# Queries as two single-pass products of a rounded copy and its rest, penalties in single passes, and the first gate sums behind tile 17 of the z projection

## The chip, the cores and the metric

The kernel runs on one core of a Trainium2 chip. The core has TensorE (PE in the profile), VectorE (DVE), ScalarE (ACT), GpSimd (POOL), SyncE (SP, which here only issues transfers) and 16 DMA engines. The metric is the device time of one execution in microseconds (us); less is better.

## The reference

One inference step of one decoder layer, for a prompt of 256 rows and for 8 samples with 2,048 past tokens each. Cut to what matters:

```python
z = x @ w_in                        # (264 rows) x (1024 x 3072); columns q | k | v | B | C | h
# sample: keys and values of 16 pages of 128 tokens, 8 heads x 64
gate = einsum('bthd,bnhd->bthn', q, kmean)       # one number per block of 256 tokens
sel  = top_k(gate, 3)                            # attend to the 3 best blocks and the own one
s = q . k / 8 - slopes * distance;  s = -inf outside sel
att = softmax(s) @ v
mix = concat(att, B * dwconv3(C * h)) @ w_out
x1 = LayerNorm(alpha * x + mix)
u  = dwconv3(x1 @ w_ffn_up);  a, g = split(u)
y  = LayerNorm(alpha * x1 + (silu(a) * g) @ w_ffn_down)
```

Outputs are y, the new keys and values and the last rows of both convolutions.

## The kernel before, in words

Five programs, one for each engine, are written out by hand. Within an engine or a queue everything happens in the written order, and semaphores with thresholds tie the engines together, so a wait holds back all that is written behind it.

**z projection.** TensorE computes 24 tiles of z, `z_tile(0)` to `z_tile(23)`. A tile is 8 fp32 products of 128x264; a fp32 product shows as two matmuls in the profile. Four tiles share one chunk of `w_in` (2 MB), and the chunks take turns in the two halves of `wring`. ScalarE copies each tile out of PSUM (`s_ze`) and issues the next chunk when a half is free. From tile 8 on two PSUM banks take turns, so `z_tile(n)` waits for the copy of tile n-2.

**Sample queries.** TensorE computes the query rows `qs` of the 8 samples first. `query(b)` spreads sample b's row over all partitions, as a product of `qs` (512 columns) with a column of the selector `sel`, and ScalarE copies it to `qb`. Queries 2 to 7 stand in pairs behind tiles 0, 1 and 2.

**Key scan.** A "page group" j = 0 to 31 is four pages (1 MB) of keys in one of four slots of `KV`; j = 4b + s belongs to sample b. VectorE multiplies it with the query (`multiply`, L907) and sums over each head (`reduce`, L917). `scan(j)` is `multiply(j+1)` and then `reduce(j)`. For the groups in `POOLED` GpSimd does the last page's product (`multiply_page`, L541), and except for the groups in `WHOLE` ScalarE sums the last page (`sum_products`, L643). SyncE loads group j into its slot when group j-4 has been multiplied.

**Gate and softmax of samples 0 to 3** (`x = 0`), woven into z tiles 16 to 22. It is a chain that goes back and forth between engines: `gate_sums(0)` on TensorE (16 products with one column each, L1439, needs `reduce(15)`), `gate_penalties(0)` on VectorE (L958 to L966), `penalties(0)` on TensorE (two fp32 products of 512 columns, L1450 and L1452), `token_max(0)` on VectorE (L975, L976), `max_rows(0)`, `max_diagonal(0)`, `max_broadcast(0)`, `shifted_scores(0)`, `exponentials(0)` on ScalarE, `probability_sums(0)` on VectorE, `denominators(0)` on TensorE and then VectorE, and the weights `Pw` for the values. Samples 4 to 7 (`x = 1`) follow the same steps near 193 us.

**Prompt heads.** `head_scores(i)` (TensorE), `head_masked(i)` (VectorE), `head_exp(i)`, `head_normalise(i)` (ScalarE), `head_transposes(i)` and `head_outputs(i)` for head pairs i = 0 to 3 stand between the z tiles as well.

**SyncE's queue.** It issues the key pages, then value pages in between. The first value group that lies in `wring` waits for all 24 z tiles, because the last chunk of `w_in` lies there:

```python
elif i >= 4:
    sp.wait_ge(s_z, 24)
```

In the written order, this wait stands behind `load_keys(6, 0)` (group 24), and that one needs `multiply(20)` on VectorE and `multiply_page(20)` on GpSimd. Behind it stand all other keys and values, the `w_ffn_up` pieces and everything else that is loaded.

**After z.** TensorE takes up `values` (L1547), `mix_tile` and the row tiles, then `x1` and an early part of the up projection, until the last value group (31) has been used. Then x1 is split into a rounded part and its rest, and the remaining up and down projections run as three single-pass (fp32r) products for each fp32 one, to the end.

Of the kernel before, what the change touches and what calls it, by code (L numbers as in the profile page):

```python
# [59 lines left out]
def build(nc, x_prompt, x_sample, cache_k, cache_v, state_conv, state_ffn_conv, page_table,  # L60
# [13 lines left out]
    with ctx:  # L74
        def sb(name, shape, dt=F32):
            return ctx.enter_context(nc.sbuf_tensor(name, shape, dt))[:]

        def at(name, offset, shape, dt=F32R):
            return nc.alloc_sbuf_tensor_at(name, shape, dt, offset=offset)[:]

        def sem(name):
            return ctx.enter_context(nc.semaphore(name))
# [14 lines left out]
        lnT = sb("lnT", [P, 16])  # L97
        xsP = sb("xsP", [P, KT, 32])
        uptail = sb("uptail", [P, NTAIL, 2 * FT])
        cst = sb("cst", [P, 2 * FT, NS])  # L100
        smax = sb("smax", [P, 32])
        msum = sb("msum", [P, 32])
# [3 lines left out]
        G8 = sb("G8", [32, NBLK])  # L106
        beats = sb("beats", [32, NBLK, 2, NBLK])
        pen = sb("pen", [32, NBLK])
        penx = sb("penx", [32, NBLK, 32])
        tri = sb("tri", [32, NBLK * NBLK])  # L110
        sel = sb("sel", [P, NS])
        qkT = sb("qkT", [P, 4, NS])
# [7 lines left out]
        shift = sb("shift", [P, 3])  # L120
        nhalf = sb("nhalf", [P, 3])
        alibi = sb("alibi", [P, NPAGE * NH])

        T = sb("T", [P, 2, NPAGE + 1, 4 * NH])
        wlo0_mem = nc.sbuf_base - NS * (NPAGE + 1) * NH * 4
# [9 lines left out]
        hT0 = sb("hT", [P, 2, 3 * P])  # L135
        cu = sb("cu", [P, NPR])
        old = at("old", nc.sbuf_base - NPR * 4, [P, 2 * FT, NS], F32)
        ct = sb("ct", [P, NPR])
        dist = sb("dist", [P, 3 * P])
        cs2 = at("cs2", nc.sbuf_base - 3 * P * 4, [P, 2 * FT, NS], F32)  # L140
# [59 lines left out]
        first_rows = ((P, ps[:, 2:4, :], 0, rows[:, 0, :]), (P, ps[:, 0:2, :], P, rows[:, 1, :]),  # L200
                      (NS, ps[0:NS, 4:6, :], NPR, srows[0:NS, :]))

        s_id = sem("ident_landed")
        s_xs = sem("x_sample_landed")
        s_sel = sem("selector_landed")
        s_pad = sem("x_sample_padding")
# [303 lines left out]
        def _(pool):  # L510
# [18 lines left out]
                chain(nc.gpsimd.tensor_tensor(dst, old_rows(0, 2 * FT, k), taps(0, 2 * FT, k), ALU.mult))  # L529
            chain(nc.gpsimd.tensor_tensor(cst, cst, old, ALU.add))  # L530
            pool.sem_inc(s_cst, 1)

            def multiply_page(j):
                b, s = divmod(j, SLOTS)
                pool.wait_ge(s_qb, b + 1)
                pool.wait_ge(s_kv[s], 16 * GP * b + 16 * GP)
                if j - 2 in WHOLE:
                    pool.wait_ge(s_red, j - 1)
                else:
                    pool.wait_ge(s_reda, act_sums(j - 1))  # L540
                nc.gpsimd.tensor_tensor(prod[:, j % 2, GD * DA:GP * DA], kv[:, s, GD, :], qb[:, b, :], ALU.mult).then_inc(s_kpool, 1)  # L541
# [23 lines left out]
            nc.gpsimd.tensor_copy(vsT, zT[:, 8:12, NPR:R]).then_inc(s_vst, 1)  # L565
            multiply_page(19)
            for t in range(4):
                if t in (1, 2, 3):
                    multiply_page(19 + t)
                pool.wait_ge(s_ze, 20 + t + 1)  # L570
                nc.gpsimd.tensor_tensor(catT[:, 4 + t, 0:NPR], catT[:, 4 + t, 0:NPR], zT[:, 12 + t, 0:NPR], ALU.mult).then_inc(s_cvT, 1)
            nc.gpsimd.tensor_tensor(catT[:, 4:8, NPR:R], cus, zT[:, 12:16, NPR:R], ALU.mult).then_inc(s_cvT, 1)

            for j in range(23, 30):
                multiply_page(j)
# [48 lines left out]
        def _(act):  # L624
# [131 lines left out]
            head_exp(3)  # L756
            z_tile(19)
            act.dma_start(wo_mix, wout[:, 4:KT, :]).then_inc(s_wom, 16)
            head_normalise(3)
            exponentials(0)  # L760
            z_tile(20)
            sum_products(19)
            kv_rows(1)
            z_tile(21)
            kv_rows(3)
            z_tile(22)
            head_transposes(2)
# [114 lines left out]
        def _(dve):  # L882
# [436 lines left out]
        def _(pe):  # L1319
# [39 lines left out]
            def query(b):  # L1359
                if b >= 2:  # L1360
                    pe.wait_ge(s_qb, b - 1)
                nc.tensor.matmul(ps[:, 4 + b % 2, :], sel[:, b:b + 1].to_broadcast([P, P]), qs,  # L1362
                                 start=True, stop=True).then_inc(s_qbps, 1)

            def z_tile(n, between=None):
                c, i = divmod(n, 4)
# [76 lines left out]
            def penalties(x):  # L1443
                pe.wait_ge(s_pen, x + 1)
                if x == 0:
                    pe.wait_ge(s_ownT, 4)
                else:
                    pe.wait_ge(s_r1, KT)
                distances = alibi.rearrange("p (g o h) -> p g o h", g=NPAGE, o=1).to_broadcast([P, NPAGE, 4, NH])
                nc.tensor.matmul(ps[:, 4, :], ident, distances, start=True, stop=False)  # L1450
                blocks = penx.rearrange("q k (o m) -> q k o m", o=1).to_broadcast([32, NBLK, 2, 32])
                nc.tensor.matmul(ps[:, 4, :], ones[0:32, :], blocks, start=False, stop=True).then_inc(s_penps, 1)  # L1452

            def max_rows(x):
                pe.wait_ge(s_pm, x + 1)
# [51 lines left out]
            head_transposes(1)  # L1507
            z_tile(16)
            head_scores(3)
            gate_sums(0)  # L1510
            z_tile(17)
            penalties(0)
            z_tile(18)
            max_rows(0)
            z_tile(19, lambda: max_broadcast(0))
            z_tile(20)
            denominators(0)
            kv_rows(1)
            z_tile(21)
            kv_rows(3)  # L1520
            head_transposes(2)
            z_tile(22)
            kv_rows(5)
            head_outputs(0)
            head_outputs(1)
# [323 lines left out]
```

## Time and profile before

| | |
|---|---|
| Time, median of 3 runs | 460.01 us (459.68 to 460.74) |
| The profiled execution: time | 460.07 us |
| its span in the profile | 458.3 us |
| Busy: PE, PEld | 424.6 us (93%), 346.1 us (76%) |
| Busy: DVE, ACT, POOL | 291.0 us (64%), 183.9 us (40%), 109.6 us (24%) |
| Moved by DMA | 124.85 MB, mean 272 GB/s |
| Granted TensorE clock, mean | 0.971 |

PE is the matmul part of TensorE and PEld its weight loads. Busy shares are means over a kernel with three stages: the z projection and key scan (to about 135 us), the value stage (to about 257 us), and the feed-forward part. A matmul's duration in a timeline includes its way through the array; where they follow one another, the distance between starts is what one costs. "PEclk" is the granted clock as a share of full speed. A DMA share of 1.0 or a little above means that all 16 engines are busy.

### The profile page before, as it was taken

To read this page: it belongs to the slowest core of one execution; us is meant where nothing else is said; L and a number is where in the kernel's file an instruction comes from. 1 tells how busy PE (TensorE), PEld (TensorE's weight loads), DVE (VectorE), ACT (ScalarE), POOL (GpSimd) and SP (SyncE) were. 2 spreads that over 40 slices of the span, in tenths; PEclk is the share of its full clock that TensorE was granted. 3 is DMA by queue.
4 is the path that set the end of the run, shared out by engine and by line. 5 is a ranking of instruction groups with operands and counts; after the bars stand their busy time and mean duration, and the time that the engine had idled before them with its cause. 6 is when DMAs were issued, how large, how long until landed. Compare 5 with 4: busy or idle time off the path is not lost.

```text
span 458.3 us, 8227 instructions
## 1 busy us (share of the span) xinstructions
PE 424.6 (93%) x2905; PEld 346.1 (76%) x2905; DVE 291.0 (64%) x368; ACT 183.9 (40%) x698; POOL 109.6 (24%) x134
## 2 busy tenths in 40 slices
PE   5999999979999996799999699999999989999990
PEld 5677888867867663665565359999999989999990
DVE  0388999898896676933442146566666875443527
ACT  1567658733537332401120043555544365324201
POOL 1002223982443552000000434211111122000002
PEclk9999999979999998899999799999999999999997
DMA  8999999899939999999999943666666674958102
GB/s 306 373 343 371 387 387 386 310 393 391 396 140 354 386 395 387 387 387 386 386 377 386 321 144 95 183 185 185 180 172 173 176 202 130 247 143 221 36 1 94
DMA packets 108332, 124.85 MB, mean 272 GB/s; under 512 B 5744, under 2 KB 64841, under 8 KB 108283
## 3 DMA queue, kind: packets, MB, share of 16 engines
q1 hardware_dynamic: 100994, 107.55, 70.9%
q10 hardware_dynamic: 7296, 16.78, 10.1%
q8 instruction: 23, 0.38, 0.4%
q14 instruction: 19, 0.15, 0.1%
HBM read 121.90 MB, written 2.61 MB: 272 GB/s over the span
## 4 chain that ended last, share of the span: by engine, by line
PE 67%; SPq 9%; issue 7%; DMA 6%; DVE 4%; ACT 3%; POOL 3%; POOLq 1%; DVEq 0%; ACTq 0%
PE ps L1377 19%; PE ps L1736 11%; PE ps L1737 11%; PE ps L1738 11%; SPq L345 8%; PE ps L1327 4%; PE ps L1641 3%; DMA KV<-in_cache_k 2%; DMA KV<-in_cache_v 2%; PE ps L1362 2%; PE ps L1547 2%; PE ps L1335 1%; POOL x1l L590 1%; PE ps L1720 1%; DVE wlo L1150 1%
## 5 line engine op out<-in xcount | busy, mean ns | idle before, releaser
L1150 DVE TENSOR_TENSOR wlo<-KV,whi 128x2048 fp32r<-128x2048 f32 (+1 forms) x24 | 61.8, 2575 | 58.9 <-ACT whi L813 30.2
L1377 PE MATMUL ps<-xT,wring 128*128 128x264 f32 x384 | 92.1, 396 | 0.0
L1377 PEld LDWEIGHTS ps<-xT,wring 128*128 128x128 f32 x384 | 73.5, 195 | 15.9 <-issue 3.0
L1736 PE MATMUL ps<-x1h,whi 128*128 128x264 f32 x256 | 73.8, 288 | 1.6 <-issue 1.6
L907 DVE TENSOR_TENSOR qk<-KV,qk 128x1536 f32<-128x1536 f32 (+1 forms) x32 | 65.2, 2040 | 12.9 <-DMA KV<-in_cache_k 6.9
L1737 PE MATMUL ps<-x1l,whi 128*128 128x264 f32 x256 | 72.6, 283 | 0.0
L1738 PE MATMUL ps<-x1h,wlo 128*128 128x264 f32 x256 | 72.5, 283 | 0.0
L643 ACT ACTIVATE qk<-qk 128x64 f32<-128x64 f32 x216 | 51.7, 245 | 18.5 <-POOL qk L541 18.0
L917 DVE TENSOR_REDUCE T<-qk 128x24 f32<-128x1536 f32 (+1 forms) x32 | 58.4, 1827 | 0.0
L1736 PEld LDWEIGHTS ps<-x1h,whi 128*128 128x128 f32 x256 | 48.2, 188 | 3.4 <-issue 3.2
L1736 PE MATMUL ps<-fh,whi 128*128 128x264 f32 x176 | 50.2, 285 | 0.3 <-DVE wlo L1150 0.2
L1737 PE MATMUL ps<-fl,whi 128*128 128x264 f32 x176 | 49.9, 284 | 0.0
L1738 PE MATMUL ps<-fh,wlo 128*128 128x264 f32 x176 | 49.8, 283 | 0.0
L1737 PEld LDWEIGHTS ps<-x1l,whi 128*128 128x128 f32 x256 | 48.2, 188 | 0.0
L1738 PEld LDWEIGHTS ps<-x1h,wlo 128*128 128x128 f32 x256 | 48.0, 188 | 0.0
L813 ACT ACTIVATE whi<-KV 128x2048 fp32r<-128x2048 f32 x16 | 30.6, 1915 | 39.5 <-PE ps L1738 39.5
L541 POOL TENSOR_TENSOR qk<-KV,qk 128x512 f32<-128x512 f32 x19 | 33.7, 1774 | 39.7 <-DMA KV<-in_cache_k 21.5
L643 ACT ACTIVATION_READ_ACCUMULATOR qk<-qk 128x1 f32 x216 | 41.2, 191 | 0.0
L1130 DVE SCALAR_TENSOR_TENSOR U<-ps,stT,U 128x255 f32<-128x255 f32 (+1 forms) x84 | 34.5, 474 | 4.5 <-ACT uptail L803 4.5
L1736 PEld LDWEIGHTS ps<-fh,whi 128*128 128x128 f32 x176 | 33.2, 188 | 0.8 <-DVE wlo L1150 0.5
L1737 PEld LDWEIGHTS ps<-fl,whi 128*128 128x128 f32 x176 | 33.1, 188 | 0.0
L1738 PEld LDWEIGHTS ps<-fh,wlo 128*128 128x128 f32 x176 | 33.0, 188 | 0.0
(200 smaller groups left out, 585.9 us busy)
## 6 DMA issues: line engine op xcount, KB each, us to landing
KV<-in_cache_k SPq DMA_DIRECT2D x128, 256.0 KB, 7.2
KV<-in_w_ffn_up SPq DMA_DIRECT2D x32, 512.0 KB, 5.2
KV<-in_cache_v SPq DMA_DIRECT2D x60, 256.0 KB, 8.6
wring<-in_cache_v SPq DMA_DIRECT2D x56, 256.0 KB, 7.4
wring<-in_w_in ACTq DMA_DIRECT2D x6, 2048.0 KB, 15.0
KV<-in_w_ffn_down SPq DMA_DIRECT2D x8, 1408.0 KB, 7.0
zbuf<-in_cache_v SPq DMA_DIRECT2D x12, 256.0 KB, 6.3
zbuf<-in_w_ffn_up SPq DMA_DIRECT2D x3, 1024.0 KB, 10.9
```

Of the source, the lines that this page charges most:

```text
L345: sp.dma_start(dst[:, g, :], pages[bass.ds(ids[g], 1)].rearrange("o t d -> (o t) d")).then_inc(landed, 16)
L541: nc.gpsimd.tensor_tensor(prod[:, j % 2, GD * DA:GP * DA], kv[:, s, GD, :], qb[:, b, :], ALU.mult).then_inc(s_kpool, 1)
L643: ins = nc.scalar.activation(x, x, ACT.Copy, accum_out=T[:, b // 4, GP * s + GD, b % 4 * NH + h:b % 4 * NH + h + 1])
L813: nc.scalar.activation(whi[s][:, 0:UNIT], w2[s][:, 0:UNIT], ACT.Copy).then_inc(s_hi, 1)
L907: nc.vector.tensor_tensor(prod[:, j % 2, 0:n * DA].rearrange("p (g d) -> p g d", g=n), kv[:, s, 0:n], q, ALU.mult).then_inc(s_kused, 1)
L917: nc.vector.tensor_reduce(dst, prod[:, j % 2, 0:n * DA].rearrange("p (g h d) -> p g h d", h=NH, d=DH), AX.X, ALU.add).then_inc(s_red, 1)
L1130: nc.vector.scalar_tensor_tensor(out, bank[:, 0:n], tap(u + a * FT, k), out, ALU.mult, ALU.add)\
L1150: nc.vector.tensor_tensor(wlo[s][:, 0:n], w2[s][:, 0:n], whi[s][:, 0:n], ALU.subtract).then_inc(s_lo, 1)
L1377: ins = nc.tensor.matmul(ps[:, z_bank(n), 0:R], w[:, k, i * P:(i + 1) * P], xT[:, k, :], start=k == 0, stop=k == KT - 1)
L1736: nc.tensor.matmul(out, wh[k], xh[k], start=k == 0, stop=False)
L1737: nc.tensor.matmul(out, wh[k], xl[k], start=False, stop=False)
L1738: ins = nc.tensor.matmul(out, wl[k], xh[k], start=False, stop=k == n - 1)
```

## The change

It has four parts.

1. **Queries 2 to 7** are computed as two single-pass (fp32r) products instead of one fp32 product. VectorE rounds `qs` to `qsr[:, 0]`, computes the rest `qsr[:, 1]`, and rounds the selector to `selr`. Queries 0 and 1 stay as they were.
2. **Penalties** (both times) are two single-pass products with `identr`, `alibir` and `onesr`, which GpSimd makes before its first page product. The new waits are `s_idr` and a higher threshold of `s_qs`.
3. **TensorE's order** in z tiles 16 to 22: `gate_sums(0)` moves behind tile 17, `penalties(0)` behind tile 18, `max_rows(0)` into the middle of tile 20, `max_broadcast(0)` behind tile 20 and `denominators(0)` behind tile 22.
4. **ScalarE's and GpSimd's orders** follow: ScalarE takes tile 20 and `kv_rows(1)` ahead of `head_normalise(3)` and `exponentials(0)`, and `head_transposes(2)` and `sum_products(19)` ahead of tile 22. GpSimd's page products 20 to 22 each move one gating step back.

```diff
         def multiply_page(j): ...
+            pool.wait_ge(s_id, 16)
+            nc.gpsimd.tensor_copy(identr, ident).then_inc(s_idr, 1)
+            nc.gpsimd.tensor_copy(onesr, ones[0:32, 0:1]).then_inc(s_idr, 1)
+            pool.wait_ge(s_const, 16 * 8)
+            nc.gpsimd.tensor_copy(alibir, alibi).then_inc(s_idr, 1)
...
             for t in range(4):
-                if t in (1, 2, 3):
-                    multiply_page(19 + t)
+                if t >= 2:
+                    multiply_page(18 + t)
...
+            multiply_page(22)
...
             nc.vector.tensor_copy(qs, ps[:, 7, :]).then_inc(s_qs, 1)
+            nc.vector.tensor_copy(qsr[:, 0, :], ps[:, 7, :]).then_inc(s_qs, 1)
+            dve.wait_ge(s_qs, 2)
+            nc.vector.tensor_tensor(qsr[:, 1, :], ps[:, 7, :], qsr[:, 0, :], ALU.subtract).then_inc(s_qs, 1)
+            dve.wait_ge(s_sel, 16)
+            nc.vector.tensor_copy(selr, sel).then_inc(s_qs, 1)
...
+                pe.wait_ge(s_qs, 4)
+                pick = selr[:, b:b + 1].to_broadcast([P, P])
+                nc.tensor.matmul(ps[:, 4 + b % 2, :], pick, qsr[:, 0, :], start=True, stop=False)
+                nc.tensor.matmul(ps[:, 4 + b % 2, :], pick, qsr[:, 1, :], start=False, stop=True).then_inc(s_qbps, 1)
...
-                nc.tensor.matmul(ps[:, 4, :], ident, distances, start=True, stop=False)
+                nc.tensor.matmul(ps[:, 4, :], identr, distances, start=True, stop=False)
...
-                nc.tensor.matmul(ps[:, 4, :], ones[0:32, :], blocks, start=False, stop=True).then_inc(s_penps, 1)
+                nc.tensor.matmul(ps[:, 4, :], onesr.to_broadcast([32, P]), blocks, start=False, stop=True).then_inc(s_penps, 1)
```

TensorE from `head_scores(3)` to the head transposes behind tile 21, as it stands before. A row is line, instruction, output<-inputs, shape and how many in a row; 8 products `ps<-xT,wring` are one z tile, `ones,T` are the gate sums, `alibi` and `penx` the penalties, `smax` is `max_rows`, `dg` is `max_broadcast` and `msum` is `denominators`:

```order
L1439 MATMUL ps<-ones,T 32x1 x16
L1377 MATMUL ps<-xT,wring 128x264 x8
L1450 MATMUL ps<-alibi,ident 128x512
L1452 MATMUL ps<-penx,ones 128x512
L1377 MATMUL ps<-xT,wring 128x264 x8
L1327 MATMUL ps<-ident,smax 32x128
L1377 MATMUL ps<-xT,wring 128x264 x4
L1460 MATMUL ps<-dg,ones 128x32
L1377 MATMUL ps<-xT,wring 128x264 x12
L1464 MATMUL ps<-msum,ones 128x32
L1327 MATMUL ps<-ident,zbuf 128x128 x4
L1377 MATMUL ps<-xT,wring 128x264 x8
```

The same stretch of TensorE in the changed kernel, down to the denominators behind tile 22:

```order
L1399 MATMUL ps<-xT,wring 128x264 x8
L1461 MATMUL ps<-ones,T 32x1 x16
L1399 MATMUL ps<-xT,wring 128x264 x8
L1473 MATMUL ps<-alibir,identr 128x512
L1475 MATMUL ps<-penx,onesr 128x512
L1399 MATMUL ps<-xT,wring 128x264 x12
L1343 MATMUL ps<-ident,smax 32x128
L1399 MATMUL ps<-xT,wring 128x264 x4
L1483 MATMUL ps<-dg,ones 128x32
L1343 MATMUL ps<-ident,zbuf 128x128 x4
L1399 MATMUL ps<-xT,wring 128x264 x8
```

Each step of the gate chain now has one more z tile ahead of it, half a tile more for the maximum, and the denominators (not in this piece) come two tiles and a half later, behind tile 22.

ScalarE from the copy of tile 19 on, before; `zbuf<-ps` is the copy of a z tile, `rows<-ps` a key or value row tile, `hrec` is `head_normalise(3)`, `T<-T` is `exponentials(0)`, and `qk,T<-qk` is `sum_products(19)`:

```order
L758 DMA wring<-in_w_out 128x4x1024
L670 ACTIVATE hs<-hs,hrec 128x128
L670 ACTIVATE hs<-hs,hrec 128x256
L670 ACTIVATE hs<-hs,hrec 128x128
L670 ACTIVATE hs<-hs,hrec 128x256
L686 ACTIVATE T<-T 128x544
L648 ACTIVATE zbuf<-ps 128x264
L643 ACTIVATE qk,T<-qk 128x64 x8
L655 ACTIVATE rows<-ps 128x512
L648 ACTIVATE zbuf<-ps 128x264
L655 ACTIVATE rows<-ps 128x512
L648 ACTIVATE zbuf<-ps 128x264
```

And in the changed kernel:

```order
L769 DMA wring<-in_w_out 128x4x1024
L659 ACTIVATE zbuf<-ps 128x264
L666 ACTIVATE rows<-ps 128x512
L681 ACTIVATE hs<-hs,hrec 128x128
L681 ACTIVATE hs<-hs,hrec 128x256
L681 ACTIVATE hs<-hs,hrec 128x128
L681 ACTIVATE hs<-hs,hrec 128x256
L697 ACTIVATE T<-T 128x544
L659 ACTIVATE zbuf<-ps 128x264
L666 ACTIVATE rows<-ps 128x512
L689 ACTIVATE hT<-ps 128x384 x2
L654 ACTIVATE qk,T<-qk 128x64 x8
```

Tile 20's copy no longer waits behind the exponentials, and `sum_products(19)` now comes behind the head transposes.

## Rows read from the trace of the kernel before

**Rows 1.** Chain that ended last: start us, length us, engine or queue, line.

```profile
23.88 1.72 PE ps L1362 x4
25.59 3.56 PE ps L1377 x16
...
94.70 2.37 issue
97.07 1.75 PE ps L1439 x32
98.82 6.35 PE ps L1377 x16
105.17 0.86 PE ps L1450 x2
106.03 1.05 PE ps L1452 x2
...
134.82 0.33 SPq L345
```

**Rows 2.** Windows of core 0: stretch, length, five engines' busy time, PEclk, DMA share, GB/s.

```profile
88.00:92.50 4.50, 4.50 (x25) 3.90 (x24) 4.50 (x5) 3.92 (x20) 4.15 (x5) 1.00 0.64 188
97.07:98.82 1.75, 1.75 (x33) 1.74 (x33) 1.75 (x3) 1.49 (x4) 1.65 (x2) 0.54 1.06 390
98.82:105.17 6.35, 6.35 (x18) 5.05 (x18) 6.18 (x15) 0.00 (x0) 5.52 (x12) 0.59 1.04 400
190.80:193.90 3.10, 1.27 (x37) 1.15 (x40) 2.62 (x3) 0.00 (x0) 0.00 (x0) 1.00 1.06 389
127.00:137.50 10.50, 9.62 (x71) 7.16 (x73) 10.23 (x6) 4.29 (x12) 5.40 (x4) 1.00 0.34 121
137.50:256.00 118.50, 109.37 (x637) 69.27 (x629) 64.84 (x93) 32.47 (x189) 20.05 (x10) 0.97 1.05 383
```

**Rows 3.** Timeline of SyncE's queue, the last key loads before the value pages.

```profile
117.18 9.35 SPq L345 DMA_DIRECT2D KV<-in_cache_k  x8
```

**Rows 4.** Timeline of TensorE, single-pass products of the up projection.

```profile
281.88 0.29 PE L1736 MATMUL ps<-x1h,whi 128*128 128x264 f32 x1
...
282.24 0.28 PE L1736 MATMUL ps<-x1h,whi 128*128 128x264 f32 x1
```

**Rows 5.** Timeline of VectorE: start, length, line; in brackets idle before and releaser.

```profile
16.33 0.69 DVE L895 COPY qs<-ps 128x512 f32<-128x512 f32 x1 [9.37 <-PE ps L1352]
19.03 4.49 DVE L907 TENSOR_TENSOR qk<-KV,qk 128x2048 f32<-128x2048 f32 x2 [2.01 <-ACT qk L631]
...
85.89 1.14 DVE L930 SCALAR_TENSOR_TENSOR hs<-dist,slope,ps 128x384 f32<-128x384 f32 x2 [1.79 <-PE ps L1387]
...
95.23 1.74 DVE L917 TENSOR_REDUCE T<-qk 128x24 f32<-128x1536 f32 x1
...
102.93 0.41 DVE L966 TENSOR_TENSOR penx<-pen,ident 32x256 f32<-32x256 f32 x1
...
108.74 1.07 DVE L976 TENSOR_REDUCE smax<-T 128x32 f32<-128x544 f32 x1
...
120.94 0.35 DVE L995 RECIPROCAL rden<-ps 128x32 f32<-128x32 f32 x1
121.32 1.49 DVE L1014 TENSOR_TENSOR Pw<-T,rden 128x128 f32<-128x128 f32 x2
122.73 1.74 DVE L907 TENSOR_TENSOR qk<-KV,qk 128x1536 f32<-128x1536 f32 x1
```

**Rows 6.** DMA issues from 39 to 41 us: KB each, us to landing.

```profile
wring<-in_w_in ACTq DMA_DIRECT2D x1, 2048.0 KB, 14.8
```

**Rows 7.** Timeline of GpSimd: two page products.

```profile
103.86 2.49 POOL L541 TENSOR_TENSOR qk<-KV,qk 128x512 f32<-128x512 f32 x2
...
147.11 2.85 POOL L541 TENSOR_TENSOR qk<-KV,qk 128x512 f32<-128x512 f32 x1 [3.90 <-DMA KV<-in_cache_k]
```

**Rows 8.** Timeline of TensorE: the last value page.

```profile
256.29 1.06 PE L1547 MATMUL ps<-KV,Pw 128*32 128x512 f32 x8 [1.68 <-DMA KV<-in_cache_v]
```

More of the change, by code:

```diff
@@ L99, in build @@
         uptail = sb("uptail", [P, NTAIL, 2 * FT])
+        selr = at("selr", nc.sbuf_base - NTAIL * 2 * FT * 4, [P, NS])
         cst = sb("cst", [P, 2 * FT, NS])
@@ L108, in build @@
         pen = sb("pen", [32, NBLK])
-        penx = sb("penx", [32, NBLK, 32])
+        penx = sb("penx", [32, NBLK, 32], F32R)
         tri = sb("tri", [32, NBLK * NBLK])
@@ L122, in build @@
         alibi = sb("alibi", [P, NPAGE * NH])
+        alibir = at("alibir", nc.sbuf_base - NPAGE * NH * 4, [P, NPAGE * NH])
         T = sb("T", [P, 2, NPAGE + 1, 4 * NH])
@@ L129, in build @@
         OM = sb("OM", [P, 2, DA])
+        qsr = at("qsr", nc.sbuf_base - 2 * DA * 4, [P, 2, DA])
         hT1 = at("hT1", nc.sbuf_base - 2 * DA * 4, [P, 2, 3 * P], F32)
@@ L137, in build @@
         old = at("old", nc.sbuf_base - NPR * 4, [P, 2 * FT, NS], F32)
+        identr = at("identr", nc.sbuf_base - (NPR - 4 * NS) * 4, [P, P])
+        onesr = at("onesr", nc.sbuf_base - (NPR - 4 * NS - P) * 4, [32, 1])
         ct = sb("ct", [P, NPR])
@@ L201, in build @@
                       (NS, ps[0:NS, 4:6, :], NPR, srows[0:NS, :]))
-        s_id = sem("ident_landed")
+        s_id, s_idr = sem("ident_landed"), sem("exact_copies")
         s_xs = sem("x_sample_landed")
@@ L758, in _ @@
             act.dma_start(wo_mix, wout[:, 4:KT, :]).then_inc(s_wom, 16)
+            z_tile(20)
+            kv_rows(1)
             head_normalise(3)
             exponentials(0)
-            z_tile(20)
-            sum_products(19)
-            kv_rows(1)
             z_tile(21)
             kv_rows(3)
+            head_transposes(2)
+            sum_products(19)
             z_tile(22)
-            head_transposes(2)
             kv_rows(5)
@@ L1361, in query @@
                     pe.wait_ge(s_qb, b - 1)
-                nc.tensor.matmul(ps[:, 4 + b % 2, :], sel[:, b:b + 1].to_broadcast([P, P]), qs,
-                                 start=True, stop=True).then_inc(s_qbps, 1)
+                if b < 2:
+                    nc.tensor.matmul(ps[:, 4 + b % 2, :], sel[:, b:b + 1].to_broadcast([P, P]), qs,
+                                     start=True, stop=True).then_inc(s_qbps, 1)
+                    return
+                pe.wait_ge(s_qs, 4)
+                pick = selr[:, b:b + 1].to_broadcast([P, P])
+                nc.tensor.matmul(ps[:, 4 + b % 2, :], pick, qsr[:, 0, :], start=True, stop=False)
+                nc.tensor.matmul(ps[:, 4 + b % 2, :], pick, qsr[:, 1, :], start=False, stop=True).then_inc(s_qbps, 1)
             def z_tile(n, between=None):
@@ L1448, in penalties @@
                     pe.wait_ge(s_r1, KT)
-                distances = alibi.rearrange("p (g o h) -> p g o h", g=NPAGE, o=1).to_broadcast([P, NPAGE, 4, NH])
-                nc.tensor.matmul(ps[:, 4, :], ident, distances, start=True, stop=False)
+                pe.wait_ge(s_idr, 3)
+                distances = alibir.rearrange("p (g o h) -> p g o h", g=NPAGE, o=1).to_broadcast([P, NPAGE, 4, NH])
+                nc.tensor.matmul(ps[:, 4, :], identr, distances, start=True, stop=False)
                 blocks = penx.rearrange("q k (o m) -> q k o m", o=1).to_broadcast([32, NBLK, 2, 32])
-                nc.tensor.matmul(ps[:, 4, :], ones[0:32, :], blocks, start=False, stop=True).then_inc(s_penps, 1)
+                nc.tensor.matmul(ps[:, 4, :], onesr.to_broadcast([32, P]), blocks, start=False, stop=True).then_inc(s_penps, 1)
             def max_rows(x):
@@ L1509, in _ @@
             head_scores(3)
+            z_tile(17)
             gate_sums(0)
-            z_tile(17)
+            z_tile(18)
             penalties(0)
[L1513 to L1517, printed above, removed]
+            z_tile(19)
+            z_tile(20, lambda: max_rows(0))
+            max_broadcast(0)
             kv_rows(1)
@@ L1522, in _ @@
             z_tile(22)
+            denominators(0)
             kv_rows(5)
```

## The prediction

> **What bounds the kernel now.** I read the chain that ended last first, then the windows around the places it named, then the timelines of SyncE, VectorE and GpSimd there. The chain runs through TensorE from the start to the last z tile, and passes at 134.82 us to SyncE's queue, when the value pages go out [rows 1]. SyncE had finished its key loads at 117.18 + 9.35 = 126.53 us [rows 3]: 8.3 us of pause, in which it waits for z tile 23. The DMA engines drain meanwhile: from 127 to 137.5 us their share is 0.34, and from 137.5 to 256 us it is 1.05 throughout [rows 2]. So the value stage is bound by transfers that can't start before tile 23 is done, and at its end TensorE waits 1.68 us for the last value page [rows 8]. What follows starts when that page is used. Time that TensorE gains before tile 23 should therefore reach the end of the kernel, as long as SyncE, VectorE and the DMA engines keep up.
>
> On TensorE's way to tile 23 there is one expensive place. It stands 2.37 us from 94.70 us on, takes 1.75 us for the gate sums, and then 6.35 us for tile 17, where another tile takes 3.56 us [rows 1]. The granted clock is 0.54 and 0.59 in these two stretches [rows 2], mostly the lower of the two levels (1.2 against 2.4 GHz). Ahead of it lay a stall and 16 one-column products. The stall is the wait for `reduce(15)`, which ends at 95.23 + 1.74 = 96.97 us [rows 5].
>
> **Queries.** A pair of fp32 queries takes 1.72 us [rows 1], 0.43 us per 512 columns and recorded half. The new pair is four single-pass products of 512 columns. The nearest row is the 264-column fp32r product: three of them take 282.24 - 281.88 = 0.36 us, 0.12 us each [rows 4]. Scaled by columns that is 0.23 us, so 0.93 us for the pair and 0.79 us saved; three pairs save 2.4 us. I take 2.3. Bounds: if a single-pass product took as long as a whole fp32 query (0.86 us), the three pairs would cost 5.2 us more; 0.21 us each would save 2.6 us. The fp32r rows make the first end unlikely.
>
> The Trainium skill says in "FP8 and Floating Point Precision", TensorE Precision Notes, that true fp32 goes through the array in four passes. By that, two passes replace four and a pair would save 0.86 us; the rows say slightly less, 0.79.
>
> **What pays for them.** VectorE does three more operations ahead of the first `multiply`: a copy and a subtraction of 512 columns like the one of 0.69 us, and a tiny one. It stood idle for 2.01 us there [rows 5]. Two times 0.69 and 0.2 us for the tiny one and the wait make 1.6 us, which fits with 0.4 us to spare. If not, all of VectorE's scan is later by the rest, at most 1 us. GpSimd's three copies come while it waits for page group 9. I cost both at nothing. The copy of chunk 2 of `w_in` takes 14.8 us to land [rows 6] and is issued when tile 3 is copied; both its issue and tile 8, which needs it, move by the same amount, so whatever slack there is stays.
>
> **Tile 17 ahead of the gate sums.** After the queries TensorE arrives at this place at 94.70 - 2.3 = 92.4 us. It does tile 17 at full clock, to 96.0 us. VectorE is earlier too: at 85.89 us it waited 1.79 us for `head_scores(2)` [rows 5], which now comes 2.3 us earlier. So `reduce(15)` ends at 95.2 us, and the gate sums don't wait. At full clock they take at most 1.27 us, which is all of TensorE's busy time in the window where the second set runs [rows 2]. That window has also a pause ahead of the sums and a clock of 1.00, so I expect no fall of the clock. To 97.2 us.
> - Saved: the stall of 2.37 us, 0.5 us of gate sums, and 6.35 - 3.56 = 2.79 us of tile 17.
>
> **Penalties.** 0.86 + 1.05 = 1.91 us [rows 1] become two single-pass products, 0.5 us: 1.4 saved. (The second time, near 197 us, the DMA engines set the pace and it is worth nothing.) But now they wait: tile 18 ends at 100.8 us, and VectorE has `penx` at 103.34 - 1.79 = 101.55 us [rows 5], since `reduce(16)` stands ahead of it there. New stall 0.8 us. Then tile 19 and half of tile 20, to 107.4 us; the token maximum is there at 109.81 - 1.79 = 108.0 us [rows 5]. New stall 0.6 us. Tiles 20 to 23 and what stands between them are the same work as before. `denominators(0)` is late now. From the end of the penalties at 107.08 us to 134.82 us were 27.7 us [rows 1], six tiles of 3.56 us and 6.3 us of small products and gaps. From the maximum at 108.0 us to the end of tile 22 stand two and a half tiles, 8.9 us, and about a third of the small ones: 119.0 us, and with the product itself 119.4 us. VectorE, which took the sums up at 120.94 us, then needs 0.35 + 1.49 us, and reaches `multiply(20)` at 121.4 instead of 122.73 us [rows 5]: 1.3 us earlier only.
>
> **Sum to tile 23.** 2.3 + 2.37 + 0.5 + 2.79 + 1.4 - 0.8 - 0.6 = 8.0 us: tile 23 is done at 126.8 instead of 134.8 us. SyncE must have got there: it needs `multiply(20)`, now done at about 123.2 us, and then 2 us of issues, 125.2 us. Just in time.
>
> **From there to the end.** GpSimd and VectorE hold nothing back yet, so count the DMA engines. Their idle capacity from 127 to 137.5 us is 10.5 x (1 - 0.34/1.05) = 7.1 us, and in the dip from 88 to 92.5 us it is 4.5 x (1 - 0.64/1.05) = 1.8 us [rows 2], of which most goes, because ScalarE issues chunk 5 some 1.5 us earlier. If only the first were to be had, the gain would end at 7.1 us; with both, all 8.0 us arrive. I take 7.7. VectorE is then the late one: at the pause's end it is only 1.3 us ahead of before, so 6.7 us behind relative to the loads. But from 137.5 to 256 us it is busy 64.84 of 118.5 us [rows 2], so 53.7 us are free to catch up in, and the slots that it empties are asked for one after the other, a group at a time. The profiled execution took 460.07 us, 0.06 over the median: 460.01 - 7.7 = **452.3 us**.
>
> **Rivals.**
> - *The clock falls anyway* (0.16). The gate sums are still 16 one-column products, and stalls of 0.8 and 0.6 us follow. If tile 18 then runs like tile 17 before, it costs 2.79 + 0.5 us, less the 0.8 us stall that it swallows: 2.5 us, so 454.8 us. For it: rows 2, clock 0.54 in the sums. Against: the second set at 1.00. The Trainium skill ("TensorE: Matmul & The Clock Gate", HAM oscillation) warns that idle gaps between bursts bring the slow level back; the trace agrees for the gap of 2.37 us, and it doesn't for the pause near 191 us.
> - *The woven engines are late* (0.17). ScalarE copies tile 18 behind `sum_products(17)`, which waits for a GpSimd product, and tile 20 needs that copy. GpSimd's product takes 1.25 us (2.49 for two) or 2.85 us beside VectorE's [rows 7]. By my sum that product ends at 103.86 - 2.3 + 1.25 = 102.8 us, the sum on ScalarE takes some 2 us more and the copy 0.4 us, and tile 20 starts at 105.6 us: 0.4 us of slack. One or two such delays, and a late key page on VectorE, cost 1.5 to 4 us: 453.8 to 456.3 us. The skill's "SBUF — State Buffer" describes an exclusive port shared by these two engines; rows 7 agree.
> - *VectorE bounds the value stage* (0.05). Then only its own 1.3 us or less arrive: 458.7 to 460 us. It would need a queue behind `residual` or the key slots that lasts to 180 us. Its idle time speaks against it.
> - *Slower, by the clock staying low* (0.04). If from the gate sums on it stays low, each z tile costs 2.79 us more. For tiles 18 to 22 that is 14 us, and with 0.5 us for the sums and 1.4 us of swallowed stalls 13.1 us against 8.0 gained: 465.1 us. It decides from a little over three tiles on; before it lasted for less than two.
> - *More than forecast* (0.06): no stall at the penalties and the small gaps gone, under 450.7 us.
>
> **How the numbers follow.** My forecast, 450.7 to 453.8 us, has 0.52. The range of 8 in 10 adds the clock's return and most of the late engines: 450.6 to 456.0 us. No change can be told from one under 0.2% (0.9 us). Faster: 0.52 + 0.16 + 0.17 + 0.06, and half of the VectorE case: 0.93. Same: 0.03. Slower: 0.04.
>
> **What would show it.** Right: SyncE's first value page into `wring` at 126 to 128 us; the clock at 1.00 from 92 to 107 us; query pairs of 0.9 us; TensorE stalls of about 1 us ahead of the penalties and in tile 20; a DMA share near 1.05 from 129 us on. Wrong: the queue at 126 us waiting for VectorE or GpSimd and not for TensorE; DMA share below 1 between 130 and 245 us; VectorE idle for less than 10 us from 130 to 175 us; tile 18 at 6 us.

## The result, and the profile after

The changed kernel takes 453.08 us (median of 4 runs, 451.86 to 454.41) against 459.85 us: 0.987 of the time, 95% interval 0.9833 to 0.9908. Measured again, beside further runs of the kernel before, it was 452.32 against 458.51 us, 0.9864 (0.9834 to 0.9894). The profiled execution took 452.91 us, its span is 451.1 us. The forecast was 452.3 us, range 450.6 to 456.0.

The chain that ended last, of the changed kernel (start, length, what):

```profile
37.87 11.98 DMA KV<-in_cache_k
49.93 2.29 DVE qk L923
...
95.65 1.74 DVE T L933
97.53 1.76 DVE qk L923
99.28 2.20 DVE T L933
102.79 0.42 DVE penx L982
103.26 0.49 PE ps L1473
103.75 0.43 PE ps L1475
104.17 5.54 PE ps L1399 x24
```

Before, this stretch ran through TensorE [rows 1]. Now it runs through a key page and then VectorE's scan up to `penx` at 103.2 us, and joins TensorE only at the penalties (L1473), on which it stays until tile 23. VectorE is the path to the gates.

TensorE there, and at the queries and the last value page (in brackets idle before, and releaser):

```profile
23.60 0.40 PE L1385 MATMUL ps<-qsr,selr 128*128 128x512 f32 x1
23.83 0.39 PE L1384 MATMUL ps<-qsr,selr 128*128 128x512 f32 x1
...
93.23 3.83 PE L1399 MATMUL ps<-xT,wring 128*128 128x264 f32 x16
97.49 1.15 PE L1461 MATMUL ps<-ones,T 128*32 128x1 f32 x32 [0.43 <-issue]
98.57 3.83 PE L1399 MATMUL ps<-xT,wring 128*128 128x264 f32 x16
103.26 0.49 PE L1473 MATMUL ps<-alibir,identr 128*128 128x512 f32 x1 [0.86 <-DVE penx L982]
103.68 0.50 PE L1475 MATMUL ps<-penx,onesr 32*128 32x512 f32 x1
...
109.75 0.28 PE L1343 MATMUL ps<-ident,smax 128*32 128x128 f32 x1
...
249.70 1.94 PE L1570 MATMUL ps<-KV,Pw 128*32 128x512 f32 x8 [1.67 <-DMA KV<-in_cache_v]
```

Single-pass products start 0.23 us apart. The stall of 2.37 us is 0.43 us. Tile 17 takes 3.83 us, like tile 18. The windows (columns as in [rows 2]) show that the clock did not fall between 92 and 107 us, and that the pause of the DMA engines, a share of 0.34 over 10.5 us in [rows 2], is nearly gone:

```profile
92.00:107.00 15.00, 13.71 (x89) 10.44 (x89) 14.63 (x23) 5.11 (x33) 12.97 (x16) 1.00 1.04 397
97.49:98.64 1.15, 1.15 (x33) 1.14 (x33) 1.15 (x2) 1.14 (x4) 1.06 (x2) 1.00 1.03 397
98.60:103.20 4.60, 3.80 (x18) 2.92 (x16) 4.43 (x10) 0.67 (x2) 4.02 (x8) 1.00 1.03 398
120.00:130.50 10.50, 9.62 (x73) 7.36 (x75) 9.23 (x10) 5.96 (x28) 3.79 (x5) 1.00 0.93 318
130.50:249.50 119.00, 109.74 (x635) 70.38 (x632) 72.03 (x97) 32.83 (x189) 20.23 (x11) 0.96 1.05 383
```

VectorE's timeline and SyncE's:

```profile
43.61 2.93 DVE L923 TENSOR_TENSOR qk<-KV,qk 128x2048 f32<-128x2048 f32 x1 [0.20 <-DVE T L933]
...
49.93 2.29 DVE L923 TENSOR_TENSOR qk<-KV,qk 128x2048 f32<-128x2048 f32 x1 [1.73 <-DMA KV<-in_cache_k]
...
85.90 1.11 DVE L946 SCALAR_TENSOR_TENSOR hs<-dist,slope,ps 128x384 f32<-128x384 f32 x2
...
108.61 1.09 DVE L992 TENSOR_REDUCE smax<-T 128x32 f32<-128x544 f32 x1
...
121.94 1.75 DVE L923 TENSOR_TENSOR qk<-KV,qk 128x1536 f32<-128x1536 f32 x1
```

```profile
115.11 11.60 SPq L350 DMA_DIRECT2D KV<-in_cache_k  x8
127.95 3.95 SPq L350 DMA_DIRECT2D wring<-in_cache_v  x8
```

The value pages go out at 127.95 us, 6.87 us earlier than at 134.82 [rows 1]; the last one is used 6.59 us earlier (256.29 in [rows 8]), the span is 7.2 us shorter, and the medians differ by 6.8 us. But `reduce(15)` ends at 97.39 us, not earlier than before (96.97), and the token maximum at 109.70 us (before 108.74 + 1.07 = 109.81 us [rows 5]).

### The profile page after: what moved, and what is told of

Read it like the earlier page. It is cut to its first block, busy times and chain, and to the rows that moved or that the text cites. A ratio compares the mean times of both kernels' runs of the same rounds, so it can differ in the third digit from the quotient of the medians.

```text
span 451.1 us, 8231 instructions
## 1 busy us (share of the span) xinstructions
PE 417.2 (92%) x2901; PEld 343.5 (76%) x2901; DVE 293.4 (65%) x371; ACT 183.8 (41%) x698; POOL 110.1 (24%) x137
## 4 chain that ended last, share of the span: by engine, by line
PE 51%; DVE 15%; SPq 10%; issue 9%; DMA 8%; ACT 3%; POOL 2%; POOLq 1%; DVEq 0%; ACTq 0%
PE ps L1759 12%; PE ps L1760 11%; PE ps L1761 11%; SPq L350 8%; DVE qk L923 5%; DVE T L933 5%; PE ps L1399 4%; DMA KV<-in_cache_k 4%; PE ps L1664 4%; PE ps L1343 3%; DMA KV<-in_cache_v 2%; PE ps L1570 2%; DMA rows<-in_x_prompt 2%; POOL x1l L601 1%; PE ps L1743 1%
## 5 line engine op out<-in xcount | busy, mean ns | idle before, releaser
L1399 PE MATMUL ps<-xT,wring 128*128 128x264 f32 x384 | 89.6, 388 | 0.0
L1399 PEld LDWEIGHTS ps<-xT,wring 128*128 128x128 f32 x384 | 71.7, 190 | 13.6 <-issue 1.7
L923 DVE TENSOR_TENSOR qk<-KV,qk 128x1536 f32<-128x1536 f32 (+1 forms) x32 | 67.4, 2109 | 10.2 <-DMA KV<-in_cache_k 6.3
L551 POOL TENSOR_TENSOR qk<-KV,qk 128x512 f32<-128x512 f32 x19 | 31.4, 1655 | 39.6 <-DMA KV<-in_cache_k 16.1
```

Of the source, the lines that this page charges most:

```text
L923: nc.vector.tensor_tensor(prod[:, j % 2, 0:n * DA].rearrange("p (g d) -> p g d", g=n), kv[:, s, 0:n], q, ALU.mult).then_inc(s_kused, 1)
L1399: ins = nc.tensor.matmul(ps[:, z_bank(n), 0:R], w[:, k, i * P:(i + 1) * P], xT[:, k, :], start=k == 0, stop=k == KT - 1)
```

## Experiments

Each time stands beside runs of the kernel before that were made together with it. "Pages out" is when SyncE starts the first value page in the profiled execution; the last value page is used 121.1 to 122.2 us after it in every kernel. This column is one execution each. The changed kernel has 127.95 and 128.07 us in two of them. Where the clock falls, it can scatter more: tile 17 alone took 6.35 us in one execution of the old order and 5.51 us in another.

| kernel | us | before, us | ratio (95%) | pages out, us |
|---|---|---|---|---|
| order only | 454.32 | 459.08 | 0.9891 (0.9855 to 0.9927) | 129.08 |
| queries only | 459.24 | 459.08 | 0.9996 (0.9971 to 1.0021) | 136.10 |
| penalties only | 458.90 | 459.08 | 1.0003 (0.9978 to 1.0028) | 134.41 |
| before, stall filled | 458.67 | 459.08 | 0.9993 (0.9971 to 1.0014) | 134.53 |
| tile 17 moved only | 461.43 | 458.51 | 1.0064 (1.0041 to 1.0088) | 136.73 |
| tail of the order only | 457.75 | 458.51 | 0.9977 (0.9953 to 1.0002) | 132.16 |
| changed, fp32 queries | 452.83 | 458.51 | 0.9863 (0.9838 to 0.9887) | 128.59 |
| changed, again | 452.32 | 458.51 | 0.9864 (0.9834 to 0.9894) | 128.07 |
| changed, chunk 2 later | 452.49 | 459.00 | 0.9850 (0.9826 to 0.9873) | 127.96 |
| changed, fp32 penalties | 453.88 | 459.00 | 0.9894 (0.9868 to 0.9921) | 128.92 |
| changed, late maximum | 455.43 | 459.00 | 0.9938 (0.9915 to 0.9962) | 130.45 |
| steps inside tiles | 451.15 | 459.00 | 0.9832 (0.9809 to 0.9855) | 125.78 |

**The parts alone.** First the whole new order, without single-pass products (and without the copies that VectorE and GpSimd make for them):

```diff
-                nc.tensor.matmul(ps[:, 4 + b % 2, :], pick, qsr[:, 0, :], start=True, stop=False)
-                nc.tensor.matmul(ps[:, 4 + b % 2, :], pick, qsr[:, 1, :], start=False, stop=True).then_inc(s_qbps, 1)
+                nc.tensor.matmul(ps[:, 4 + b % 2, :], sel[:, b:b + 1].to_broadcast([P, P]), qs, start=True, stop=True).then_inc(s_qbps, 1)
...
-                nc.tensor.matmul(ps[:, 4, :], identr, distances, start=True, stop=False)
+                nc.tensor.matmul(ps[:, 4, :], ident, distances, start=True, stop=False)
```

> The new order of TensorE, ScalarE and GpSimd alone; queries and penalties stay fp32. Theory (the order takes away the stall, and with it the low clock): TensorE arrives at 94.7 us as before, tile 17 takes about 3.6 us instead of 6.35, the gate sums come at 98.3 us without a wait and at full clock, and 2.37 + 2.79 + 0.5 = 5.7 us are saved less a few tenths of new stalls: the kernel takes about 454.5 us (453.9 to 455.2). Rival (the clock falls at the gate sums wherever they stand, and tile 18 takes 6 us): 2.4 us are saved, about 457.5 us. Second rival (the single passes carry most of the gain): under 3 us saved, 457 us or more.

454.32 us, 4.8 us faster: the order carries most of the gain. TensorE's timeline of it:

```profile
94.79 3.83 PE L1383 MATMUL ps<-xT,wring 128*128 128x264 f32 x16
98.55 1.17 PE L1445 MATMUL ps<-ones,T 128*32 128x1 f32 x32
```

Tile 17 and the sums follow each other without a wait, the clock is 1.00 from 94.8 to 105.4 us, and the value pages go out 5.7 us earlier, the 2.37 + 2.79 + 0.5 us of the expectation. Neither rival held: tile 18 takes 3.83 us. Then the two others, each put alone into the kernel before (its part of the diff shown above the prediction):

> The single-pass queries alone, in the old order and with fp32 penalties. Theory (in the old order the gate sums wait for VectorE's last reduce, which is not earlier): TensorE arrives about 1.5 to 2.3 us earlier and waits that much longer, reduce(15) ends between 96.5 and 97.5 us, tile 17 still takes about 6 us, and the time stays within 0.6 us of before. Rival (the saved TensorE time counts as a plain sum): 2.3 us faster, about 457.6 us. If the longer stall brings the clock lower still, it is up to 1 us slower.

> The single-pass penalties alone, in the old order and with fp32 queries. Theory (in the old order nothing waits at the penalties, TensorE is the path): 1.91 us become 0.5 to 0.9 us (the clock is low there), so 1.0 to 1.4 us are saved, about 458.8 us. Rival (GpSimd's three copies take the shared port from VectorE and make its scan late, so that reduce(15) ends after 97.0 us): the stall ahead of the gate sums grows by 0.4 us or more, and what is left is under 1 us: 459.1 to 460 us.

Both are worth nothing that can be measured (459.24 and 458.90 against 459.08 us; the intervals leave room for 1.3 and 1.0 us of gain). TensorE's timeline, of queries only (first two rows) and of penalties only:

```profile
70.91 0.95 PE L1337 MATMUL ps<-ident,zbuf 128*128 128x128 f32 x4 [2.09 <-ACT rows L660]
...
98.33 1.81 PE L1455 MATMUL ps<-ones,T 128*32 128x1 f32 x32 [2.52 <-issue]
```

```profile
96.77 1.15 PE L1449 MATMUL ps<-ones,T 128*32 128x1 f32 x32 [2.42 <-issue]
97.84 5.51 PE L1387 MATMUL ps<-xT,wring 128*128 128x264 f32 x16
103.00 0.58 PE L1461 MATMUL ps<-alibir,identr 128*128 128x512 f32 x1
...
110.25 0.28 PE L1337 MATMUL ps<-ident,smax 128*32 128x128 f32 x1 [2.48 <-DVE smax L986]
```

With the queries alone TensorE does not come earlier to the gate sums, as was expected, but 1.1 us later (95.81 against 94.70 us). It loses 2.09 us to ScalarE's key rows at 70.91 us, and ScalarE had itself waited 3.18 us for VectorE's part of a prompt head. Behind that wait the clock fell too:

```profile
70.91:73.70 2.79, 2.79 (x15) 2.02 (x15) 2.25 (x2) 2.79 (x23) 0.70 (x1) 0.53 1.02 358
```

In the kernel with penalties alone, the penalties' saving comes back as a wait of 2.48 us for the token maximum. Before, that wait was not there, but TensorE turned the maximum at 110.67 us, only 0.9 us after VectorE had it. That sets a new theory beside the sum of the prediction: the maximum is a fixed point, which VectorE has between 109.2 and 110.4 us whatever TensorE does (so in twelve of the fourteen profiled executions; in queries only at 111.8 us, since VectorE itself is late there, and in one kernel below that makes it late), and TensorE gains by what it has done ahead of it.

**The stall filled.** This tells idleness from the one-column sums as what the clock falls after:

```diff
+            pe.wait_ge(s_rowcp, 3)
+            for i in range(8):
+                nc.tensor.matmul(ps[:, 5, 0:P], ident, ident, start=True, stop=True)
             gate_sums(0)
```

> The kernel before, with eight fp32 products of 128 columns (into a bank that the gate sums overwrite; their results are used nowhere) in the stall ahead of the first gate sums. Theory (the idle stall is what the clock falls after): the granted clock stays near 1.00 from 94.7 to 102 us, the sums take about 1.2 us and tile 17 about 3.6 us, so some 3.3 us are saved: about 456.7 us. Rival (the 16 one-column products make the clock fall by themselves): the time is unchanged or a few tenths longer, tile 17 still takes 6.35 us.

TensorE's timeline of it:

```profile
94.20 2.05 PE L1512 MATMUL ps<-ident 128*128 128x128 f32 x16
96.85 1.15 PE L1439 MATMUL ps<-ones,T 128*32 128x1 f32 x32 [0.59 <-issue]
97.92 3.83 PE L1377 MATMUL ps<-xT,wring 128*128 128x264 f32 x16
103.05 1.13 PE L1450 MATMUL ps<-alibi,ident 128*128 128x512 f32 x2 [1.30 <-DVE penx L966]
...
110.36 0.28 PE L1327 MATMUL ps<-ident,smax 128*32 128x128 f32 x1 [1.37 <-DVE smax L976]
```

On the clock the theory was right: with the stall filled, sums and tile 17 run at the high level. On the time it was wrong, 458.67 us: of the 3.2 us saved (the sums 1.15 instead of 1.75 us, tile 17 3.83 instead of 6.42), 1.30 are waited for the penalty rows and 1.37 for the maximum.

**The halves of the order.** Tile 17 ahead of the sums, and nothing else:

```diff
-            gate_sums(0)
             z_tile(17)
+            gate_sums(0)
             penalties(0)
```

> The kernel before with one pair of steps exchanged on TensorE: tile 17 ahead of the first gate sums; all that follows stays in its old order, fp32 throughout. Theory T (VectorE's token maximum, done at about 109.8 us in every kernel run so far, is a fixed point for TensorE; only what TensorE has left to do behind it counts): the clock stays at 1.00 and tile 17 takes 3.6 us, but TensorE then waits about 3 us for the penalty rows and about 1 us for the token maximum, and tile 23 is done 0.3 to 0.8 us earlier than before: 458.3 to 459.5 us against about 459.1 us. Rival (the plain sum of this place, 2.37 + 0.5 + 2.79 us, reaches the end): about 453.5 us.

It is slower by 2.9 us (1.9 us at the value pages), which neither theory gave. Timeline of TensorE, and the window of the penalties:

```profile
98.16 1.17 PE L1439 MATMUL ps<-ones,T 128*32 128x1 f32 x32
103.52 2.08 PE L1450 MATMUL ps<-alibi,ident 128*128 128x512 f32 x2 [4.19 <-DVE penx L966]
105.53 2.07 PE L1452 MATMUL ps<-penx,ones 32*128 32x512 f32 x2
107.53 5.19 PE L1377 MATMUL ps<-xT,wring 128*128 128x264 f32 x16
```

```profile
103.50:107.50 4.00, 3.98 (x4) 1.00 (x4) 4.00 (x9) 2.02 (x16) 2.81 (x4) 0.50 1.03 393
```

The stall moved to the penalties and is 4.19 us there; behind it the clock is 0.50, the lower level throughout. Tile 18 between sums and penalties is therefore not a detail: it covers this wait. The other half, as a difference to the kernel with the order only:

```diff
+            gate_sums(0)
             z_tile(17)
-            gate_sums(0)
-            z_tile(18)
             penalties(0)
+            z_tile(18)
             z_tile(19)
             z_tile(20, lambda: max_rows(0))
```

> The other half of the new order alone: gate sums ahead of tile 17 as before, and the token maximum inside tile 20, the denominators behind tile 22, with ScalarE and GpSimd in their new order; fp32 throughout. Theory T: the stall and the low clock remain, so TensorE ends the penalties at about 107 us and has two and a half tiles to do ahead of the token maximum, which it therefore reaches at about 116 us instead of 110.7 us, with correspondingly less left: no more than 0.7 us faster, 458.2 to 459.3 us. Rival (the later place of the maximum carries the gain by itself): 455 us or less. A loss is possible, if VectorE, now late with the first Pw, holds the key loads back: up to 462 us.

457.75 us: between nothing and 2.1 us by its interval. (Its profiled execution was among its fastest, 455.67 us.) In it TensorE turns the maximum at 113.97 us, 4.0 us after VectorE had it. Its value pages go out 2.7 us earlier, but 2.0 of these TensorE has already at the end of the penalties, ahead of all that differs, most of it because the clock fell later in this execution. So the halves gave +2.9 and -0.8 us, and together -4.8 us.

**The fixed point, made later.** In the changed kernel:

```diff
+                if x == 0:
+                    for i in range(2):
+                        chain(nc.vector.tensor_reduce(smax, T[:, x].rearrange("p g m -> p m g"), AX.X, ALU.max))
                 nc.vector.tensor_reduce(smax, T[:, x].rearrange("p g m -> p m g"), AX.X, ALU.max).then_inc(s_pm, 1)
```

> The changed kernel with VectorE's reduction to the first token maximum done three times instead of once, 2.2 us more on VectorE right ahead of that point; nothing else moves. Theory T (in the changed kernel the maximum is a point that TensorE waits at): TensorE stands about 2.0 us ahead of the turn of the maximum, its clock may fall behind that stand, and tile 23 is done 2.0 to 3.5 us later, 454.3 to 455.8 us. Rival (TensorE has slack there, since it is itself the path): under 0.7 us later, 453 us or less.

TensorE's timeline, and the window behind its stall:

```profile
112.26 0.28 PE L1346 MATMUL ps<-ident,smax 128*32 128x128 f32 x1 [2.26 <-DVE smax L995]
```

```profile
112.20:116.00 3.80, 3.74 (x20) 3.03 (x21) 3.39 (x8) 1.11 (x3) 0.73 (x1) 1.00 1.03 400
```

2.2 us more on VectorE are 2.50 us at the value pages, and 455.43 us. By ratio (0.9938 against 0.9864 and 0.987) that is about 3.3 us, with intervals that just don't touch. TensorE has no slack there. The clock did not fall.

**What single passes are worth in the new order.** The queries back to fp32, and in another kernel the penalties:

> The changed kernel with its queries back to fp32, order and penalties as changed. Theory T: TensorE reaches the token maximum some 0.5 to 1 us after VectorE has it instead of 0.1 us after, so 0.3 to 1.0 us are lost against the changed kernel: 453.4 to 454.1 us if that one takes 453.1. Rival (the prediction's term): 2.3 us lost, 455.4 us.

> The changed kernel with fp32 penalties and without GpSimd's three copies; queries and order as changed. Theory T (TensorE reaches the token maximum only 0.1 us after VectorE has it, so what it loses ahead of that point comes straight back): penalties of 2.0 instead of 1.0 us, tile 23 is done 0.7 to 1.3 us later than in the changed kernel (127.8 us), about 453.3 us where that one takes 452.3. Rival (the copies slow VectorE, whose waits eat the saving): no loss, or a gain of up to 0.5 us.

> The changed kernel itself, as a reference on the same chip as the three other kernels of this call: 453.1 us, and tile 23 done at 127 to 128.5 us.

The queries are worth 0.5 to 0.6 us at the value pages, and no difference in time (0.9863 against 0.9864). Even the 0.6 us are not TensorE's columns: with fp32 queries GpSimd starts its two page products at 104.50 instead of 103.72 us, VectorE has the maximum at 110.34 instead of 109.70 us, and TensorE turns it 0.05 us later in both kernels. The penalties are worth 0.9 us there (128.92 against 127.95 to 128.07), which the times allow and don't prove.

**Chunk 2 of `w_in` asked for later.** In the changed kernel ScalarE issues it behind the copies of the stack transposes:

```diff
             z_tile(3)
-            load_win(2)
...
+            load_win(2)
             for j in range(4, 8):
```

> The changed kernel, with chunk 2 of w_in asked for about 2 us later (behind ScalarE's two copies of the stack transposes), as late as before the change. Theory L (chunk 2, asked for 2.7 us earlier by the faster queries, takes DMA share from the key pages, and VectorE therefore waits 1.73 us for page group 7): that wait shrinks to under 0.5 us, reduce(15) ends at 96.2 us or earlier instead of 97.4, and tile 23 is done 0.4 to 1.2 us earlier. Rival (the lateness comes from VectorE's products running longer beside GpSimd): reduce(15) ends at 97 us or later as in the changed kernel, and the time is unchanged within 0.5 us.

VectorE's timeline:

```profile
53.11 2.29 DVE L923 TENSOR_TENSOR qk<-KV,qk 128x2048 f32<-128x2048 f32 x1 [0.68 <-DMA KV<-in_cache_k]
...
95.67 1.75 DVE L933 TENSOR_REDUCE T<-qk 128x24 f32<-128x1536 f32 x1
```

The wait for page group 7 is gone, one of 0.68 us for the next group has come, and `reduce(15)` ends at the same 97.42 us. The theory falls, and the rival's forecast held. VectorE is 0.97 us ahead of the changed kernel at 56.3 us, and 0.8 of it is gone by 61.6 us: a small product (L967) beside GpSimd's page product takes 0.87 instead of 0.18 us, another 0.12 us longer. So less waiting for key pages is not enough to make VectorE earlier.

**One step further.** If the fixed point is right, steps inside tiles should leave no stall. The maximum now also stands behind tile 20, half a tile later:

```diff
-            gate_sums(0)
-            z_tile(18)
-            penalties(0)
-            z_tile(19)
-            z_tile(20, lambda: max_rows(0))
-            max_broadcast(0)
+            z_tile(18, lambda: gate_sums(0))
+            z_tile(19, lambda: penalties(0))
+            z_tile(20)
+            max_rows(0)
             kv_rows(1)
-            z_tile(21)
+            z_tile(21, lambda: max_broadcast(0))
...
-            sum_products(17)
             z_tile(18)
+            sum_products(17)
```

> A further step of the same kind from the changed kernel: gate sums in the middle of tile 18, penalties in the middle of tile 19, the token maximum behind tile 20 and its broadcast inside tile 21, and ScalarE copies tile 18 ahead of its sum of page product 17. Theory T: the stands of 0.43 and 0.86 us ahead of sums and penalties go, TensorE never waits between 90 and 110 us, tile 23 is done 0.9 to 1.4 us earlier (about 126.6 us), and the kernel takes about 451.3 us where the changed one takes 452.3. Rival (SyncE's key loads, now behind VectorE's later multiply(20), are done after tile 23 and hold the value pages): unchanged, or up to 1 us slower.

TensorE's timeline, and SyncE's:

```profile
92.83 5.61 PE L1399 MATMUL ps<-xT,wring 128*128 128x264 f32 x24
98.37 1.17 PE L1461 MATMUL ps<-ones,T 128*32 128x1 f32 x32
99.47 3.83 PE L1399 MATMUL ps<-xT,wring 128*128 128x264 f32 x16
102.94 0.58 PE L1473 MATMUL ps<-alibir,identr 128*128 128x512 f32 x1
```

```profile
125.78 3.95 SPq L350 DMA_DIRECT2D wring<-in_cache_v  x8
```

No stall is left at these steps, the chain runs through TensorE again, and the value pages go out 2.2 us earlier than in the changed kernel, where 0.9 to 1.4 us were expected. TensorE turns the maximum at 109.33 us, only 0.4 us earlier; 1.8 us come from the half tile that no longer stands behind it. 451.15 us is the fastest of all, 1.7% under the kernel before. That it beats the changed kernel is seen in one trace (2.2 us), not proven by the times: the ratios 0.9832 and 0.9864 differ by 1.5 us, with intervals that overlap.

## Why the prediction was right, and where its sum was not

- **Bound and end of the path: right.** Every kernel uses its last value page 121.1 to 122.2 us after the first goes out, so what tile 23 gains arrives. SyncE was there in time, with less to spare than thought: its key loads ended at 115.11 + 11.60 = 126.71 us (125.2 predicted), 1.2 us ahead of the value pages. Predicted was a small loss to the DMA engines (8.0 to 7.7 us); measured 6.87 to 6.59 us.
- **Queries: the product's price right, its worth wrong.** Rows 0.23 us apart make 0.92 us a pair (0.93 predicted). VectorE's extra operations fitted, with 0.61 us of its wait left (0.4 predicted). But TensorE came to tile 17 at 93.23, not 92.4 us: 1.14 us went into a wait at 69.97 us for ScalarE's key rows, and ScalarE had waited 2.23 us for VectorE. Of 2.3 us in the sum, 0.5 to 0.6 us reached the value pages.
- **The step that failed: "VectorE is earlier too ... `reduce(15)` ends at 95.2 us".** The wait of 1.79 us for `head_scores(2)` did vanish, but VectorE had lost as much on the way and started there at 85.90 us (85.89 before). It started its product at 43.61 us 0.70 us earlier than before, but that took 2.93 us instead of 2.29, beside GpSimd (2.90 us without GpSimd's three casts, so these are not the cause). Then it waited 1.73 us for page group 7, and was 1.46 us later than before. Another 0.4 us went into a product at 81.51 us (2.67 us instead of 2.29). The one at 88.27 us took 2.77 instead of 2.28 us, so that `reduce(15)` ended at 97.39 us. In queries only it was 98.23 us. That an engine which waits at a late place will be earlier when that wait goes was the error: VectorE was held earlier on, by key pages and by its products beside GpSimd's. Which of the two decides is not shown; with chunk 2 asked for later, 1.05 us less waiting for pages changed nothing.
- **Stall, sums and tile 17: mechanism right, arithmetic incomplete.** The clock did stay at 1.00, and the stall shrank to 0.43 us. But 5.66 us saved there are not a gain by themselves. With the stall filled 3.2 of them are saved, and 0.4 us arrive, which can't be told from none (0.9971 to 1.0014); with tile 17 moved alone 2.9 us are lost. They count, so the halves and the whole of the order say, because tile 18, tile 19 and half of tile 20 then stand ahead of steps that VectorE sets.
- **New stalls:** at the penalties 0.86 us (0.8 predicted); in tile 20 none to be seen (0.6 predicted), as TensorE turns the maximum at 109.75 us, 0.05 us after VectorE has it, being itself later than thought.
- **Penalties:** 1.91 us became 0.49 + 0.43 = 0.92 us in the chain (0.5 predicted; the pair stands alone behind a wait and is not overlapped like the queries). Worth 0.9 us instead of 1.4.
- **VectorE from there:** `multiply(20)` at 121.94 us (121.4 predicted), and it was not late in the value stage. That this came so close is luck. TensorE started the denominators at 120.79 us, 1.8 us later than forecast, but the two products for `Pw` took 0.49 instead of 1.49 us, since GpSimd's page product was over by then (118.95 + 1.27 us; before it ran from 121.19 us on, beside it). In z tiles the denominators moved by two, not two and a half; two and a half is their distance to the maximum now.
- **The sum** was 8.0 us, the measured one 6.87 us. The forecast, 0.8 us under the median, was near partly by luck: the overrated queries and penalties (2.3 us too much) were partly offset by the 0.6 us of stall that was expected at the maximum and didn't come. The remaining 0.6 us of the difference can't be given to one term: the parts don't add.
- **Rivals.** The clock's return (454.8 us) and its staying low did not happen here. But the first is real: it is what tile 17 moved alone shows, one tile fewer in between. The woven engines were late on ScalarE (tile 18's copy at 106.95 us, as that rival said); in the kernel with fp32 queries it is copied at 107.73 us, and TensorE waits 0.51 us for it ahead of tile 20. VectorE did not bound the value stage (DMA share 1.05 from 130.5 to 249.5 us).

What stays open: why VectorE reaches the end of `reduce(15)` between 97.3 and 98.2 us in most kernels with single-pass queries (96.9 us with steps inside tiles) and between 96.4 and 97.5 us in those with fp32 queries. No run took away the key pages' pace, or GpSimd's products beside VectorE's.

## What to carry to other kernels

Where two engines meet at several points in a row, moving independent work ahead of the first meeting only moves the wait to the second; count for each meeting what stands ahead of it, and move the whole row together. A saving on the waiting engine is worth nothing until then: put each part in alone before crediting it. And before expecting an engine to be earlier because one of its waits goes, look upstream for what holds it there.

## What the runs showed of the hardware

- **Idle time and the clock.** Stalls of TensorE of about the same length were followed by different levels. Before, it idled from 94.70 us; the clock was 1.00 to 97.2 us, 0.1 us into the gate sums, and 0.50 from there on. Queries only did the same behind 2.52 us, and also behind a stall of 2.09 us at 70.91 us with no one-column product near (0.50 from 71.1 us on). In penalties only (2.42 us) and tail only (2.36 us) the sums ran at 1.00 and the clock fell 1.3 and 0.7 us into tile 17. And a stall of 2.48 us ahead of the maximum (penalties only) and one of 2.26 us (late maximum) left it at 1.00. With the stall filled, the same sums behind 0.59 us left it at 1.00. In the stall of 4.19 us (tile 17 moved alone) it fell at the very end, at 103.5 us. So each fall at this place had a stall of over 2 us ahead of it and the one-column sums are not needed for one; but whether a stall of 2.1 to 2.5 us brings it does not follow from its length, and no run here shows what decides. The Trainium skill, "TensorE: Matmul & The Clock Gate", HAM oscillation, tells of idle gaps between bursts as what brings the slow level back; the stalls of 2.09, 2.37, 2.52 and 4.19 us agree, those of 2.26 and 2.48 us passed without it.
- **What the lower level costs** depends on where it falls: tile 17 took 6.35 us before and in queries only, 5.51 us in penalties only and tail only, for the same 16 products.
- **VectorE beside GpSimd.** Before, GpSimd's two page products end at 103.86 + 2.49 = 106.35 us [rows 7], VectorE's next product of 1536 columns starts at 106.36 us and takes 1.75 us. With the stall filled VectorE is ready earlier: GpSimd's pair runs from 104.49 to 106.99 us, VectorE's product starts beside it at 105.77 us and takes 2.84 us. Being 0.6 us earlier, it ended 0.5 us later. At 88 us the roles change with who is first: before, VectorE's product starts at 88.29 us and takes 2.28 us, while GpSimd's operation started at 88.36 us takes 2.81 us; in the changed kernel GpSimd's starts at 88.15 us and takes 0.75 us, and VectorE's at 88.27 us takes 2.77 us.
